# First feed-forward stage on the unnormalised state, and the last expert's down products by part

## The chip, the cores and the metric

The kernel runs on one core of one Trainium2 chip. The metric is the device time of one execution in microseconds (us); smaller is better. Engine names are those of the profile: PE (TensorE, with PEld its weight loads), DVE (VectorE), ACT (ScalarE), POOL (GpSimd), SP (SyncE, which issues most DMAs).

## The reference

Two transformer blocks, each of two layers, over 256 tokens of width 1024 in fp32. Only two places of it matter here.

The first is the dense feed-forward stage of layer 0:

```python
def rmsnorm(x, g):
    y = x * lax.rsqrt(jnp.mean(x * x, axis=-1, keepdims=True) + EPS)
    return y * g

h = rmsnorm(x, norm_ffn[0])
x = x + (silu(h @ wg) * (h @ wu)) @ wd      # width D_FF = 2816
```

For one token the root is one number, so `h @ wg` is `(x * g) @ wg` times that token's root.

The second is the end of the mixture of experts in layer 1: eight experts of width 3584, each token goes to two of them, and the gated sum of the experts' down products is added to x. A fused norm (the final norm of the first block and the first norm of the second) and another dense feed-forward stage follow.

## The kernel before

The state `xT` lies with the model width in the partitions: 8 blocks k of 128 rows by T = 256 tokens. Every product of two fp32 matrices is made from parts: a value is split into a high part (ACT copies it to fp32r) and a low part (DVE subtracts the high part), and PE adds hi*hi, hi*lo and lo*hi. So weights pass through three engines: SP loads a tile into a ring of four slots, ACT makes `w_hi`, DVE makes `w_lo`, PE multiplies. The work of each engine is written out by hand in program order, and semaphores join the engines.

**A dense feed-forward stage.** `norm(n)` comes first. ACT squares the 8 blocks of xT (L774), POOL adds them in pairs (L620), PE sums over partitions with a matrix of ones into `SS`, bank 6 of PSUM (L2131), ACT makes the inverse root by a logarithm and an exponential (L759, L760) into `norm_s`. DVE multiplies each block of xT by its gains and the root to `hT` (`scaled`, L1340), ACT copies it to `a_hi` (`split_input`, L830), DVE subtracts to `a_lo` (`rest`, L1357). PE runs six matmuls into bank 7 that nobody reads (L2135) behind the sums. `head` (L754, L1312) splits the first weight tile of the stage early, `second` (L824, L1328, L1387) the second one in two halves: half 0 before the root, half 1 behind the root and the input's split.

`ffn` then runs over 22 chunks c of 128 hidden columns. PE: `up(c)` is 16 pairs of matmuls (L2510 with 512 columns, L2512 with 256) for gate and up into two banks, 4 and 5 for even c, 6 and 7 for odd c; then `down(c-1)`, 24 matmuls of 256 columns (L2106 to L2108) into banks 0 to 3. ACT in a chunk: the high part of the next up tile (L1117), of this down tile (L1126), the copy of half of the up sums out of PSUM (L1132), Silu (L1138). DVE in a chunk: the low part of the next up tile (L1691), of this down tile (L1700), in most chunks one or two blocks of a matrix-vector product for the second block of the model (L1682, one in chunks 1 to 4, two in chunks 5 to 20), the addition of the two halves of the sums (L1710), the product of Silu(gate) and up (L1717), its high and low part (L1720, L1722). `up(c+1)` needs L1691, `down(c)` needs L1722. ACT's L1117 for the tile after next stands behind the Silu of the chunk. In chunk 21 the next stage's first half tile is split (L1312) in place of L1691. The stage of this change is `ffn(0)`, behind `norm(1)`.

**The end of the experts.** The last expert has 28 chunks too, n = 196 to 223. `down(n)` is six matmuls of 512 columns (L2673): high hidden by high weights, high by low, low by high, each for two halves of the output. At the end `down(223)` waits for DVE's low part of the last down tile (L1781), ACT and DVE each copy one half of the result to `ye` (L1265, L1922), PE waits for both, `scatter_last` (L2697) multiplies by the scatter matrix, DVE adds to xT (L1927), and `norm(5)` and `ffn(2)` follow. In the chunk before the last, DVE splits both halves of the head tile of `ffn(2)`.

Of the kernel before, what the change touches and what calls it, by code (L numbers as in the profile page):

```python
# [112 lines left out]
def build(nc, x_in, wstream, astream, crow, wpool, wrouter, vectors, consts, out):  # L113
# [6 lines left out]
    with ctx:  # L120
# [143 lines left out]
        gu_copied = sem("gu_copied")  # L264
        gu_added = sem("gu_added")
        sg_ready = sem("sg_ready")
        hid_ready = sem("hid_ready")
# [57 lines left out]
        xdown_done = sem("xdown_done")  # L325
        ye_ready = sem("ye_ready")
        ys_ready = sem("ys_ready")
        ys_added = sem("ys_added")
# [169 lines left out]
        def last_bank(j):  # L498

            return 2 * ((NE - 1 + j // 2) % 2) + j % 2  # L500

# [238 lines left out]
        def _(act):  # L740
# [21 lines left out]
            def norm(n):  # L762
# [6 lines left out]
                if n == 5:  # L769
                    act.wait_ge(both_roots, 1)  # L770
                for k in range(KB):
                    if n:
                        act.wait_ge(x_ready, KB * (n - 1 - (n == 5)) + k + 1)
                    nc.scalar.activation(sq[:, k, :], xT[:, k, :], ACT.Square,  # L774
                                         scale=both[:, KB + k:KB + k + 1] if n == 5 else D ** -0.5)\
                        .then_inc(sq_ready, 1)
                if early and HEADS[n] not in FFN_STAGE:
                    head(n, 1)
                if n in SECOND_AT:
                    second(n, 0).then_inc(second_hi, 1)  # L780
# [13 lines left out]
                if n in HEADS:  # L794
                    if n == 0:
                        head(n, 1)
                    act.sem_inc(hi_ready, 1 if HEADS[n] in FFN_STAGE else 2)
                if n < 3:
                    split_input(f"n{n}", hT, h_ready, KB * n)
                elif n >= 5:  # L800
                    for k in range(KB):
                        act.wait_ge(normed, KB * (n - 5) + k + 1)
                        if k == 0:
                            act.wait_ge(mod_done, MOD_BATCH[n])
                        shift = mod[:, (n - 5) // 3, 3 * ((n - 5) % 3) * KB + k:
                                    3 * ((n - 5) % 3) * KB + k + 1]
                        nc.scalar.activation(a_hi[:, k, :], sq[:, k, :], ACT.Identity, bias=shift)\
                            .then_inc(ah_ready, 1)
                        if n == 5:
                            nc.scalar.activation(hT[:, k, :], xT[:, k, :], ACT.Square).then_inc(final_sq, 1)  # L810
# [385 lines left out]
            def moe_fast():  # L1196
# [65 lines left out]
                nc.scalar.preload_act_table_set("natural_log_exp_and_others")  # L1262
                act.wait_ge(xdown_done, NE * FX + 2)
                act.wait_ge(ye_out, ROWS_OUT[NE - 1])
                nc.scalar.activation(ye[0:CAP, 0:512], ps[0:CAP, 2 * ((NE - 1) % 2), :], ACT.Copy).then_inc(ye_ready, 1)  # L1265

# [36 lines left out]
        def _(dve):  # L1303
# [11 lines left out]
            def norm(n):  # L1315
# [6 lines left out]
                if n in (2, 6, 9):  # L1322
                    head(n, 1)
                if n in SECOND_AT:
                    stage = HEADS[n]
# [6 lines left out]
                if n == 3:  # L1332
                    up_lo_half(0, 0, 0)
                    nc.vector.memset(rt[:, 1, 0, :], 0.0).then_inc(mask_ready, 1)
                dve.wait_ge(norm_root, norm_at(n) + 1)

# [22 lines left out]

                if n == 3:  # L1360
                    for k in range(KB):
# [312 lines left out]
            def ffn(f, n):  # L1674
# [10 lines left out]
                def chunk(c, r=0, last=False, blocks=()):  # L1685
# [19 lines left out]
                    for i in blocks[:1]:  # L1705
# [4 lines left out]
                    nc.vector.tensor_tensor(sm[:, b::2, :], sm[:, b::2, :], gu[:, :, 0:T], ALU.add)\  # L1710
                        .then_inc(gu_added, 1)
                    for i in blocks[1:]:
# [120 lines left out]
            def moe_fast():  # L1833
# [38 lines left out]
                def expert(n_e, r, last=False):  # L1872

                    for c in range(FX):
# [14 lines left out]
                        elif c == FX - 2:  # L1889
                            head(5, 0)  # L1890
                            head(5, 1)
                        for half in range(2):
# [28 lines left out]
                dve.wait_ge(ye_out, ROWS_OUT[NE - 1])  # L1921
                nc.vector.tensor_copy(ye[0:CAP, 512:1024], ps[0:CAP, 2 * ((NE - 1) % 2) + 1, :]).then_inc(ye_ready, 1)  # L1922
                dve.wait_ge(ys_added, 3)
                for j in range(KB // 2):
# [172 lines left out]
        def _(pe):  # L2097
# [26 lines left out]
            def norm(n):  # L2124
# [7 lines left out]
                ins.then_inc(ss_ready, 1)  # L2132
                if n in HEADS:
                    for _ in range(6):
# [354 lines left out]
            def ffn(f, n, norm_n):  # L2489
# [3 lines left out]
                def up(c, r=0):  # L2493
# [5 lines left out]
                    for k, g in [(k, g) for k in range(KB) for g in range(2)] if c < 2 else \  # L2499
                            [(k, g) for g in range(2) for k in range(KB)]:  # L2500
                        if c == 0 and g == 0:
                            wait_head(norm_n, k)
# [129 lines left out]
            def moe_fast():  # L2632
# [29 lines left out]
                def down(n, r):  # L2662
# [13 lines left out]
                    ins.then_inc(xdown_done, 1)  # L2676

                def turn_rows(n_e, half):

# [14 lines left out]
                def scatter_last():  # L2694

                    for d in range(KB):
                        ins = mm(ps[:, last_bank(d // 2), (d % 2) * T:(d % 2 + 1) * T], ye[0:CAP, d * P:(d + 1) * P],  # L2697
                                 scatter[0:CAP, :], start=d % 2 == 0, stop=True, skip_group_check=True)
# [43 lines left out]
                expert(NE - 1, 0, last=True)  # L2742
                down(NE * FX - 1, 0)
                pe.wait_ge(ye_ready, 2 * NE)
                pe.wait_ge(ys_added, 3)
# [14 lines left out]
            mixer1(0, 0)  # L2760
            norm(1)
            ffn(0, FF, 1)
# [158 lines left out]
```

## Time and profile before

| | us |
|---|---|
| median of 3 runs (2436.2 to 2438.71) | 2437.72 |
| time of the profiled execution | 2436.53 |
| span of its profile | 2434.8 |
| PE busy | 2410.2 (99%) |
| DVE busy | 2043.3 (84%) |
| ACT busy | 1512.0 (62%) |
| POOL busy | 177.6 (7%) |

The granted TensorE clock is 0.999 over the span. The profile lists for each engine what it did and when, and for each idle stretch which engine's work ended it. Times of a timeline are counted from the start of the span. Matmuls are pipelined: the duration of one record is longer than the distance to the next one, and it is the distance that counts in a row of them. A product of two plain fp32 operands shows as two records.

### The profile page before, as it was taken

How to read it: one execution, taken by the hardware profiler on the slowest of the kernel's cores; microseconds unless marked ns; L12 is line 12 of the kernel's file. 1: busy time of each engine (PE TensorE's matmuls, PEld its weight loads, DVE VectorE, ACT ScalarE, POOL GpSimd, SP SyncE). 2: the span in 40 equal slices, each digit the busy share in tenths (PEclk: the TensorE clock that was granted, in tenths of full speed). 3: DMA queues.
4: the chain of work that ended last, by engine and by line, in shares of the span. 5: the costliest groups of instructions: out<-in, count | busy, mean ns of one | idle time of the engine just before them, and what ended most of it. 6: DMA issues, size and time to landing. Idle time of an engine off the chain costs nothing.

```text
span 2434.8 us, 43980 instructions
## 1 busy us (share of the span) xinstructions
PE 2410.2 (99%) x17072; PEld 2199.2 (90%) x17072; DVE 2043.3 (84%) x2623; ACT 1512.0 (62%) x2091; POOL 177.6 (7%) x244
## 2 busy tenths in 40 slices
PE   9999999999999999999999999999999999999999
PEld 9999999998999999899988899988999899988998
DVE  5688867999999999999998899787888888787665
ACT  5644565777787778778876544567544544566443
POOL 2211020100000000000010111011011010010000
PEclk9999999999999999999999999999999999999999
DMA  7698554999999999999998788433787687432551
GB/s 290 229 354 313 193 186 182 387 391 379 371 399 416 374 383 399 405 370 392 402 416 334 259 312 298 152 130 122 285 319 277 233 320 286 147 122 95 208 185 76
DMA packets 135662, 693.51 MB, mean 285 GB/s; under 512 B 16113, under 2 KB 16241, under 8 KB 86769
## 3 DMA queue, kind: packets, MB, share of 16 engines
q1 hardware_dynamic: 109872, 598.79, 64.8%
q0 software_dynamic: 23280, 87.17, 9.3%
q10 hardware_dynamic: 2304, 4.72, 0.5%
q8 instruction: 139, 2.28, 0.4%
q14 instruction: 67, 0.54, 0.1%
HBM read 681.98 MB, written 11.40 MB: 285 GB/s over the span
## 4 chain that ended last, share of the span: by engine, by line
PE 90%; DVE 5%; ACT 3%; issue 1%; DMA 0%; POOL 0%; DVEq 0%; ACTq 0%; SPq 0%; POOLq 0%
PE ps L2510 17%; PE ps L2106 16%; PE ps L2107 16%; PE ps L2108 16%; PE ps L2673 11%; PE ps L2512 9%; DVE w_parts L1387 1%; PE ps L2131 1%; PE ps L2135 1%; PE ps L2638 1%; DVE w_parts L1774 1%; ACT w_parts L838 1%; DMA ring<-wstream 0%; DVE xT L1409 0%; PE ps L2378 0%
## 5 line engine op out<-in xcount | busy, mean ns | idle before, releaser
L2510 PE MATMUL ps<-a_parts,w_parts 128*128 128x512 f32 x1760 | 618.7, 393 | 1.4 <-DVE a_parts L1352 1.0
L1774 DVE TENSOR_TENSOR w_parts<-ring,w_parts 128x2048 fp32r<-128x2048 f32 x221 | 506.5, 2292 | 51.0 <-ACT w_parts L1161 44.0
L2106 PE MATMUL ps<-w_parts 128*96 128x256 f32 x1792 | 501.5, 280 | 1.1 <-DVE w_parts L1774 1.0
L2108 PE MATMUL ps<-w_parts 128*96 128x256 f32 x1792 | 498.3, 278 | 0.0
L2107 PE MATMUL ps<-w_parts 128*96 128x256 f32 x1792 | 498.0, 278 | 0.0
L2512 PE MATMUL ps<-a_parts,w_parts 128*128 128x256 f32 x1760 | 492.6, 280 | 0.0
L1161 ACT ACTIVATE w_parts<-ring 128x2048 fp32r<-128x2048 f32 x221 | 422.7, 1913 | 1.5 <-DMA ring<-wstream 1.3
L2510 PEld LDWEIGHTS ps<-a_parts,w_parts 128*128 128x128 f32 x1760 | 329.8, 187 | 75.3 <-issue 3.5
L2512 PEld LDWEIGHTS ps<-a_parts,w_parts 128*128 128x128 f32 x1760 | 332.4, 189 | 0.0
L2106 PEld LDWEIGHTS ps<-w_parts 128*96 128x96 f32 x1792 | 288.0, 161 | 27.0 <-issue 17.7
L2107 PEld LDWEIGHTS ps<-w_parts 128*96 128x96 f32 x1792 | 288.4, 161 | 9.0
L2108 PEld LDWEIGHTS ps<-w_parts 128*96 128x96 f32 x1792 | 288.1, 161 | 0.0
L1781 DVE TENSOR_TENSOR a_parts<-ring,a_parts 128x1024 fp32r<-128x1024 f32 x224 | 271.3, 1211 | 0.0
L1132 ACT ACTIVATE sm<-ps 128x512 f32<-128x512 f32 x110 | 65.4, 595 | 329.4 <-PE ps L2512 329.4
L2673 PE MATMUL ps<-a_parts,hid_hi 128*96 128x512 f32 (+1 forms) x896 | 259.8, 411 | 1.1 <-DVE a_parts L1781 1.1
L1691 DVE TENSOR_TENSOR w_parts<-ring,w_parts 128x2048 fp32r<-128x2048 f32 x100 | 229.3, 2293 | 28.3 <-ACT w_parts L1117 26.9
L2108 PE MATMUL ps<-hid_hi,w_parts 128*128 128x256 f32 x880 | 249.0, 283 | 0.0
L2106 PE MATMUL ps<-hid_hi,w_parts 128*128 128x256 f32 x880 | 247.4, 281 | 1.5 <-DVE hid_lo L1722 1.5
L2107 PE MATMUL ps<-hid_lo,w_parts 128*128 128x256 f32 x880 | 248.9, 283 | 0.0
L1167 ACT ACTIVATE a_parts<-ring 128x1024 fp32r<-128x1024 f32 x224 | 235.3, 1050 | 1.1 <-PE ps L2673 1.1
L2106 PE MATMUL ps<-a_parts,w_parts 128*128 128x256 f32 x784 | 229.7, 293 | 1.1 <-DVE a_parts L1357 0.7
L2107 PE MATMUL ps<-a_parts,w_parts 128*128 128x256 f32 x784 | 221.7, 283 | 0.0
(283 smaller groups left out, 4370.1 us busy)
## 6 DMA issues: line engine op xcount, KB each, us to landing
ring<-wstream SPq DMA_DIRECT2D x378, 1024.0 KB, 7.4
ring<-wstream SPq DMA_DIRECT2D x378, 512.0 KB, 7.0
proj<-astream POOLq DMA_DIRECT2D x144, 512.0 KB, 5.5
slot_rows<-branch POOLq DMA_DIRECT2D x7, 384.0 KB, 6.2
slot_out<-slot_rows POOLq DMA_DIRECT2D x1, 2688.0 KB, 11.7
sq<-slot_rows ACTq DMA_DIRECT2D x36, 64.0 KB, 5.5
slot_out<-pT ACTq DMA_DIRECT2D x36, 64.0 KB, 5.3
vtok<-crow POOLq DMA_DIRECT2D x3, 512.0 KB, 3.8
```

Source lines behind the costliest of these rows:

```text
L1132: nc.scalar.activation(sm[:, c % 2::2, :], gu[:, :, T:2 * T], ACT.Copy).then_inc(gu_copied, 1)
L1161: nc.scalar.activation(up_hi[:, n % 2, :], ring[:, s, 0:UP], ACT.Copy).then_inc(xup_hi, 1)
L1167: nc.scalar.activation(wd_hi[:, n % 2, :], ring[:, s, UP:TILE], ACT.Copy).then_inc(xdown_hi, 1)
L1691: nc.vector.tensor_tensor(w_lo[:, (q0 + c + 1) % 2, 0:UP], ring[:, (i0 + c + 1) % NS, 0:UP], w_hi[:, (q0 + c + 1) % 2, 0:UP], ALU.subtract)\
L1774: nc.vector.tensor_tensor(up_lo[:, n % 2, :], ring[:, s, 0:UP], up_hi[:, n % 2, :], ALU.subtract).then_inc(up_used, 1)
L1781: nc.vector.tensor_tensor(wd_lo[:, n % 2, :], ring[:, s, UP:TILE], wd_hi[:, n % 2, :], ALU.subtract).then_inc(signal, 1)
L2106: mm(o, stationary[0], moving[0], start=start, stop=False, skip_group_check=True)
L2107: mm(o, stationary[0], moving[1], start=False, stop=False, skip_group_check=True)
L2108: return mm(o, stationary[1], moving[0], start=False, stop=stop, skip_group_check=True)
L2510: mm(ps[:, bank, :], hi, a_parts[:, :, k, :], start=k == 0, stop=k == KB - 1, skip_group_check=True)
L2512: ins = mm(ps[:, bank, 0:T], lo, a_hi[:, k, :], start=False, stop=k == KB - 1, skip_group_check=True)
L2673: ins = mm(ps[0:rows, bank + half, :], h[:, b, 0:rows], w[:, b, half * D // 2:(half + 1) * D // 2], start=c == 0 and i == 0, stop=c == FX ...
```

## The change

In `norm(1)`:
- ACT squares blocks 0 to 5; once all eight blocks of xT are ready it writes `a_hi` directly from xT, scaled by the norm gains; then come squares 6 and 7. DVE makes `a_lo` as xT times gains minus `a_hi`. `hT` is not written; neither waits for the root.
- PE's five matmuls of the sum over partitions move from ahead of the stage into `up(0)`, ahead of its pair (6, 0), that is behind 12 of 16 pairs. The six matmuls into bank 7 go. `up(1)`, whose banks include bank 6, waits for the root.

In `ffn(0)`, in each of 22 chunks, DVE multiplies the sums of gate and up (128x512, in place) by the root, between L1710 and Silu, with a wait for L1710's own end.

At the end of the experts:
- `down_last` replaces the last `down`: the four products with the high weights run ahead of the wait for the low part of the weights, and each half signals by itself (`xhalf_done`, `xdown_done`).
- ACT copies half 0 as soon as it is complete and PE scatters it, and waits for DVE's copy of half 1 only ahead of the fifth block. The banks of the scatter are taken in the order 2, 0, 1, 3.
- DVE's split of half 1 of the head tile of `ffn(2)` moves from the chunk before the last to behind DVE's copy of half 1.

```diff
-            return 2 * ((NE - 1 + j // 2) % 2) + j % 2
+            return (2, 0, 1, 3)[j]
...
-                for k in range(KB):
+                for k in range(6 if n == 1 else KB):
...
+                if n == 1:
+                    act.wait_ge(x_ready, KB)
+                    for k in range(KB):
+                        nc.scalar.activation(a_hi[:, k, :], xT[:, k, :], ACT.Identity, scale=V("norm_ffn", k))\
+                            .then_inc(ah_ready, 1)
+                    for k in range(6, KB):
+                        nc.scalar.activation(sq[:, k, :], xT[:, k, :], ACT.Square, scale=D ** -0.5)\
+                            .then_inc(sq_ready, 1)
...
-                if n < 3:
+                if n in (0, 2):
                     split_input(f"n{n}", hT, h_ready, KB * n)
...
-                act.wait_ge(xdown_done, NE * FX + 2)
+                act.wait_ge(xhalf_done, 1)
                 act.wait_ge(ye_out, ROWS_OUT[NE - 1])
-                nc.scalar.activation(ye[0:CAP, 0:512], ps[0:CAP, 2 * ((NE - 1) % 2), :], ACT.Copy).then_inc(ye_ready, 1)
+                nc.scalar.activation(ye[0:CAP, 0:512], ps[0:CAP, 2 * ((NE - 1) % 2), :], ACT.Copy).then_inc(ye_half, 1)
...
+                if n == 1:
+                    for k in range(KB):
+                        dve.wait_ge(ah_ready, KB * e + k + 1)
+                        nc.vector.scalar_tensor_tensor(a_lo[:, k, :], xT[:, k, :], V("norm_ffn", k), a_hi[:, k, :],
+                                                       ALU.mult, ALU.subtract).then_inc(as_ready, 1)
...
                     nc.vector.tensor_tensor(sm[:, b::2, :], sm[:, b::2, :], gu[:, :, 0:T], ALU.add)\
-                        .then_inc(gu_added, 1)
+                        .then_inc(gu_raw if f == 0 else gu_added, 1)
+                    if f == 0:
+                        if c == 0:
+                            dve.wait_ge(norm_root, norm_at(1) + 1)
+                        dve.wait_ge(gu_raw, c + 1)
+                        nc.vector.tensor_tensor(sm[:, b::2, :], sm[:, b::2, :],
+                                                norm_s[:, 1, :].unsqueeze(1).broadcast_to([P, 2, T]), ALU.mult)\
+                            .then_inc(gu_added, 1)
...
                             head(5, 0)
-                            head(5, 1)
...
                 nc.vector.tensor_copy(ye[0:CAP, 512:1024], ps[0:CAP, 2 * ((NE - 1) % 2) + 1, :]).then_inc(ye_ready, 1)
+                head(5, 1)
...
-                if n in HEADS:
+                if n in HEADS and n != 1:
                     for _ in range(6):
...
+                        if f == 0 and c == 0 and (k, g) == (6, 0):
+                            norm(1)
+                        if f == 0 and c == 1 and (k, g) == (0, 0):
+                            pe.wait_ge(norm_root, norm_at(1) + 1)
...
+                def down_last(n):
+                    b, bank = n % 2, 2 * (n // FX % 2)
+                    def product(h, w, half, stop):
+                        return mm(ps[0:CAP, bank + half, :], h[:, b, 0:CAP], w[:, b, half * D // 2:(half + 1) * D // 2],
+                                  start=False, stop=stop, skip_group_check=True)
+                    pe.wait_ge(xhid_lo, n + 3)
+                    for half in range(2):
+                        product(hid_hi, wd_hi, half, False)
+                        product(hid_lo, wd_hi, half, False)
+                    pe.wait_ge(tile_used, STARTS[MOE_STAGE] + n + 1)
+                    product(hid_hi, wd_lo, 0, True).then_inc(xhalf_done, 1)
+                    product(hid_hi, wd_lo, 1, True).then_inc(xdown_done, 1)
...
                     for d in range(KB):
+                        if d == KB // 2:
+                            pe.wait_ge(ye_ready, 2 * NE - 1)
...
-                down(NE * FX - 1, 0)
-                pe.wait_ge(ye_ready, 2 * NE)
+                down_last(NE * FX - 1)
+                pe.wait_ge(ye_half, 1)
...
             mixer1(0, 0)
-            norm(1)
             ffn(0, FF, 1)
```

## Rows read from the trace of the kernel before

**Rows 1.** The page, busy time, share and instructions of each engine.

```profile
PE 2410.2 (99%) x17072; PEld 2199.2 (90%) x17072; DVE 2043.3 (84%) x2623; ACT 1512.0 (62%) x2091; POOL 177.6 (7%) x244
```

**Rows 2.** Timeline of PE: start, us, line, tiles, count, [idle before <-what ended it].

```profile
103.86 2.75 PE L2135 MATMUL ps<-cst,ones 128*128 128x256 f32 x12
106.56 0.47 PE L2510 MATMUL ps<-a_parts,w_parts 128*128 128x512 f32 x1
...
118.02 0.28 PE L2106 MATMUL ps<-hid_hi,w_parts 128*128 128x256 f32 x1
...
120.89 0.43 PE L2510 MATMUL ps<-a_parts,w_parts 128*128 128x512 f32 x1
```

**Rows 3.** Timeline of DVE from the last additions to xT on.

```profile
101.49 0.75 DVE L1407 TENSOR_TENSOR xT<-xT,ps 128x256 f32<-128x256 f32 x2
...
105.98 0.43 DVE L1357 TENSOR_TENSOR a_parts<-hT,a_parts 128x256 fp32r<-128x256 f32 x1
...
118.48 2.29 DVE L1691 TENSOR_TENSOR w_parts<-ring,w_parts 128x2048 fp32r<-128x2048 f32 x1 [1.61 <-ACT w_parts L1117]
```

**Rows 4.** Timeline of ACT: the root, and the second tile's half 1.

```profile
104.06 0.47 ACT L759 ACTIVATE pT<-ps,vec 128x256 f32<-128x256 f32 x1 [0.43 <-PE ps L2131]
104.57 0.42 ACT L760 ACTIVATE pT<-pT 128x256 f32<-128x256 f32 x1
...
110.83 1.04 ACT L824 ACTIVATE w_parts<-ring 128x1024 fp32r<-128x1024 f32 x1
```

**Rows 5.** Timeline of ACT, eight squares scaled by per-partition values, in norm(5).

```profile
1336.13 3.41 ACT L774 ACTIVATE sq<-xT,both 128x256 f32<-128x256 f32 x8 [2.20 <-DVE xT L1927]
```

**Rows 6.** Groups of DVE by shape: busy us, mean ns | idle before.

```profile
L1433 DVE TENSOR_TENSOR sm<-sm,small 128x512 f32<-128x512 f32 x8 | 5.5, 692 | 0.3
```

**Rows 7.** Timeline of DVE, one whole round of ffn(0).

```profile
157.39 2.29 DVE L1691 TENSOR_TENSOR w_parts<-ring,w_parts 128x2048 fp32r<-128x2048 f32 x1
...
160.97 1.23 DVE L1682 SCALAR_TENSOR_TENSOR proj<-proj,vtok 128x1024 f32<-128x1024 f32 x1
...
165.10 2.29 DVE L1691 TENSOR_TENSOR w_parts<-ring,w_parts 128x2048 fp32r<-128x2048 f32 x1
```

**Rows 8.** Timeline of DVE, chunks 20 and 21 of ffn(0).

```profile
279.18 0.69 DVE L1710 TENSOR_TENSOR sm<-sm,ps 128x512 f32<-128x512 f32 x1 [0.64 <-ACT sm L1132]
...
282.17 2.29 DVE L1312 TENSOR_TENSOR w_parts<-ring,w_parts 128x2048 fp32r<-128x2048 f32 x1
...
287.61 0.69 DVE L1710 TENSOR_TENSOR sm<-sm,ps 128x512 f32<-128x512 f32 x1 [2.02 <-ACT sm L1132]
...
289.25 0.29 DVE L1720 CAST hid_hi<-sm 128x256 fp32r<-128x256 f32 x1
289.57 0.43 DVE L1722 TENSOR_TENSOR hid_lo<-sm,hid_hi 128x256 fp32r<-128x256 f32 x1
```

**Rows 9.** Timeline of PE, the start of the last down product of ffn(0).

```profile
290.06 0.38 PE L2106 MATMUL ps<-hid_hi,w_parts 128*128 128x256 f32 x1 [0.30 <-DVE hid_lo L1722]
```

**Rows 10.** Timeline of PE at the end of the experts.

```profile
1330.46 0.62 PE L2673 MATMUL ps<-a_parts,hid_lo 128*96 128x512 f32 x2
1331.68 1.15 PE L2673 MATMUL ps<-a_parts,hid_hi 128*96 128x512 f32 x4 [0.61 <-DVE a_parts L1781]
...
1334.08 3.72 PE L2697 MATMUL ps<-proj,pT 96*128 96x256 f32 x16 [0.78 <-DVE pT L1922]
```

**Rows 11.** Timeline of DVE: the low part of the last down tile.

```profile
1330.33 1.22 DVE L1781 TENSOR_TENSOR a_parts<-ring,a_parts 128x1024 fp32r<-128x1024 f32 x1
```

**Rows 12.** Windows: length, busy (x) of PE, PEld, DVE, ACT, POOL; clock; DMA.

```profile
390.00:392.00 2.00, 2.00 (x20) 2.00 (x20) 1.11 (x3) 1.00 (x2) 0.00 (x0) 0.95 0.00 0
392.00:394.00 2.00, 2.00 (x11) 1.77 (x10) 1.44 (x9) 0.60 (x1) 0.00 (x0) 0.50 0.00 0
394.00:396.00 2.00, 2.00 (x13) 1.81 (x12) 1.88 (x7) 1.50 (x3) 0.00 (x0) 0.70 0.00 0
...
2433.00:2434.80 1.80, 0.00 (x0) 0.00 (x0) 0.00 (x0) 0.00 (x0) 0.00 (x0) 0.50 0.52 200
```

More of the change, by code:

```diff
@@ L265, in build @@
         gu_added = sem("gu_added")
+        gu_raw = sem("gu_raw")
         sg_ready = sem("sg_ready")
@@ L326, in build @@
         ye_ready = sem("ye_ready")
+        xhalf_done = sem("xhalf_done")
+        ye_half = sem("ye_half")
         ys_ready = sem("ys_ready")
@@ L1334, in norm @@
                     nc.vector.memset(rt[:, 1, 0, :], 0.0).then_inc(mask_ready, 1)
-                dve.wait_ge(norm_root, norm_at(n) + 1)
+                if n != 1:
+                    dve.wait_ge(norm_root, norm_at(n) + 1)
                 def scaled(k):
@@ L1358, in rest @@
                                                 ALU.subtract).then_inc(as_ready, 1)
-                if n == 3:
+                if n == 1:
+                    dve.sem_inc(h_ready, KB)
+                elif n == 3:
                     for k in range(KB):
```

## The prediction, made before the changed kernel was run

> **What bounds the kernel now.** I read the page's busy times first. PE is busy for 99% of the span [rows 1], so an edit gains only where it closes one of PE's few gaps and loses only where it opens one. Then I read the timelines of PE, DVE and ACT side by side at the two places of the change, and DVE's through the whole stage, since the edit adds DVE work to all 22 chunks. The reader should see two things. At the head of `ffn(0)` PE is filled with unread matmuls from 103.86 until 106.56 [rows 2]; this is where the root's chain costs time. And DVE is no spare engine there: a round of a chunk with two matrix-vector blocks takes it 7.71 (157.39 to 165.10) without a pause [rows 7], while PE's round is 8.43 (L1710 from 279.18 to 287.61) [rows 8]. DVE has 0.72 to spare per round. In the later rounds the spare time shows as a wait of 0.64 ahead of L1710 [rows 8]; early in the stage there is none, as DVE is still catching up.
>
> **Part 1, the head of the stage.** The last additions to xT end at 102.24 [rows 3]. `a_hi(0)` by ACT with a per-partition scale: eight such operations take 3.41, 0.43 each in a row, about 0.5 for one alone [rows 5], so 102.8. `a_lo(0)` on DVE takes 0.43 to 0.48, so 103.3, and PE starts 0.15 after it, as it did (106.41 to 106.56) [rows 2, 3]: 103.4 instead of 106.56, 3.1 earlier. Further blocks come each 0.43, PE needs four matmuls or 0.7 for one, so it doesn't wait again. The unread matmuls cost nothing when they go; they filled a wait.
> The sums now stand inside `up(0)`: 10 records, at 2.75 for 12 about 2.3 [rows 2]. Net on PE: 0.8 to 0.9 earlier at the end of `up(0)` and `up(1)`. The 32 pairs of both took 11.46 (106.56 to 118.02), 0.358 a pair [rows 2]; the sums start behind 12 pairs at 107.7 and end at 110.0. The root takes 0.93 [rows 4] and is there at 111.0, ahead of `up(1)` at about 111.4, so the new wait on bank 6 costs nothing. But ACT's half 1 of the second tile stands behind the root: 111.0 instead of 110.83 [rows 4], 0.2 later. From there to L1691 at 118.48 [rows 3] the same ACT and DVE instructions follow in the same order, none waiting for PE, plus the new product between L1710 and Silu.
>
> **Part 2, the product.** It is 128x512, plain fp32, in place with a broadcast operand: 0.69, as L1433 of that shape [rows 6]. It waits for L1710's end: such a successor starts 0.03 after it (L1720 ends at 289.54, L1722 starts at 289.57) [rows 8]. Silu comes 0.72 later. For DVE's own round: without a wait the next one overlaps by about 0.08 (two additions in 0.75) [rows 3], so the lost overlap is 0.11 and the product occupies 0.61: again 0.72. Bounds: 0.55 with no price for the wait and full overlap, 0.85 if the two-operand read from SBUF is disturbed.
> So L1691 of chunk 1 starts at 118.48 + 0.2 + 0.72 = 119.4 and ends at 121.7; `up(2)`, at 120.89 before [rows 2], starts at 121.8. The gain of 0.9 has turned into a loss of 0.9: PE comes early and waits.
> From here DVE sets the pace. Five rounds from 118.48 to 157.39 took 38.91, and now 3.6 more; so the round that began at 157.39 [rows 7] begins at 161.9. The next 15 take 7.71 + 0.72 = 8.43, the same as PE's own. DVE's lag is therefore never made up. Its work for chunk 21 (L1312) starts at 161.9 + 15 x 8.43 = 288.35 instead of 282.17 [rows 8], and at the same time PE starts `down(20)`, which was waiting for the hidden part just finished.
>
> **Part 3, the end of the stage.** Before, DVE was ahead here by 2.02 and waited for PE and ACT [rows 8]. Now it is the last: the two subtractions take 3.58 to what follows [rows 7], so L1710 at 291.9; from L1710 to the end of L1722 it was 2.39 (287.61 to 290.00) [rows 8], now 3.11, so 295.05, and PE starts `down(21)` 0.06 later [rows 9], at 295.1 instead of 290.06. PE has nothing in between: `down(20)` of 24 matmuls (2.87, 118.02 to 120.89 [rows 2]) is over at 291.3, so it stands idle for 3.8. The residual, norm(2) and all that follows hang on this product and move with it: **+5.1**. SP's ring loads and POOL's loads also follow DVE's lag, but each slot is loaded two rounds or more before its use, so I take 0 (0 to +0.5).
>
> **Part 4, the last expert.** `down(222)`'s last two records start at 1330.46, 0.23 apart (six in 1.4), so the array is free at 1330.9; `down(223)` started at 1331.68, after L1781's end at 1331.55 [rows 10, 11]. Its four products without the low weights take 0.93, to 1331.8, by when these are there: 0.8 saved. Half 0 is complete one matmul before half 1: 0.2. ACT's and DVE's copies run in parallel as before, PE begins after the first, and half 1's is in time for the fifth block, 1.8 later (16 records in 3.72 [rows 10]). The sums of norm(5) follow on PE without a gap, ACT's squares (3.41 [rows 5]) are shorter than scatter and sums together. DVE's moved split (1.2, as L1781 [rows 11]) fits between its copy and the first addition, which waits 0.9 for PE, up to 0.3 late; it then catches up, as squares aren't last. **-1.0** (-1.2 to -0.6).
>
> **Sum.** +5.1 - 1.0 = +4.1. On the profiled execution's 2436.53 this gives 2440.6; the median of the runs shown is 1.2 above that execution, so I forecast 2437.72 + 4.1 = 2441.8. A measurement tells this kernel from no change at about 0.2%, or 4.9 us: the forecast lies inside.
>
> **A. Forecast, +4.1 (2441.8), chance 0.45.** By itself it spreads over +2.5 to +5.5.
>
> **B. The idle 3.8 ahead of `down(21)` costs TensorE's clock too.** The granted clock falls from full to half (2.4 to 1.2 GHz) in two places of the rows: at the end of the span, where PE does nothing more (0.50 from 2433 on), and from 391 to 395, behind a wait and very small matmuls [rows 12]. There the three windows lack (0.05 + 0.50 + 0.30) x 2 = 1.7 of full-speed time. Here the half level would lie over `down(21)` and norm(2)'s sums, which wait in part anyhow: +1.4, so +5.5, 2443.2, slower. For it: no other gap of the stage is as long. Against: the waits around 1331 and 1334 [rows 10], up to 0.8 each, don't say what one of 3.8 does. Chance 0.25.
> The Trainium skill ("TensorE: Matmul & The Clock Gate", section "Why this matters for your kernels") advises against idle gaps between bursts of matmuls because the clock falls back; the rule speaks against this change and for B.
>
> **C. The wait for the own result is free.** Then the product adds 0.61 to DVE's round, which is 8.32, and DVE regains 0.11 in each of 20 rounds, 2.2 in all: +1.9, 2439.6. Against it: L1722's start 0.03 behind L1720's end, where unwaited ones overlap by 0.08 [rows 3, 8]. If a round were shorter by 0.17 or more, the lag would be gone by chunk 21 and +0.6 (2438.3) is left: 0.9 at the start and the product once at the end, less 1.0. Chance of both 0.13.
> The Trainium skill ("VectorE: DVE Perf Modes", section "The DRAIN you can't avoid") says that a semaphore between chained operations costs nothing extra; by it C would hold, while the rows named there speak against it.
>
> **D. The product is hidden throughout, and both heads gain:** -0.9 - 1.0 = -1.9, 2435.8, not slower. For it: the wait of 0.64 ahead of L1710 in late rounds [rows 8] could swallow 0.64 of 0.72. Against: early there is no such wait, and L1691 ended at 120.77, 0.12 ahead of `up(2)` [rows 2, 3]. Chance 0.07.
>
> **E. The rounds grow longer than PE's.** At 0.85 for the product each of 20 rounds is 0.13 longer and PE follows DVE: +2.6, in all +6.7, 2444.4, slower. It decides from about +0.05 a round. For it: DVE and ACT now both have rounds of 8.43, and any hitch on either adds up. Against: rounds so far agree within 0.01 [rows 7, 8]. Chance 0.10.
>
> **From cases to numbers.** Slower by over 0.2%: about a fifth of A, 0.7 of B, nearly all of E: 0.37. Faster by over 0.2% needs -4.9, more than D has: 0.02. Within: 0.61. The range, 2438.3 to 2444.6, leaves out D, half of C's lower end and the worst of E.
>
> **What would show it.** In the profile after: first L2510 of the stage at about 103.4; L1691 at 119.4 and `up(2)` at 121.8; products of 0.69 with Silu right behind; L1691 starts 8.43 apart from the first round on with no wait ahead of L1710; PE idle for 3 to 4 ahead of the last `down` of the stage, at about 295; the scatter 1.0 earlier relative to `down(222)`; clock at full (A) or half (B) behind 295. I am wrong if DVE waits for PE again in the late rounds (C, D), or if rounds are over 8.5 (E).

## The result, and the profile after

The changed kernel takes 2448.12 us (median of 5 runs, 2445.7 to 2450.49), the kernel before on the same chip 2438.71 (5 runs): ratio 1.0035, 95% interval [1.0023, 1.0048], so 9.4 us slower (5.6 to 11.7). In a second comparison, at the end of the study, it was 6.7 slower. The ratios in this document are estimates of their own and not quotients of the two medians: 1.0035 is 8.5 us. I had forecast 4.1 slower and a top of 2444.6; the time lies outside.

The profiled execution took 2445.7 (span 2444.0, before 2434.8). The root's ACTIVATE of each norm is a good milestone: it has one row in every trace. Between these roots the 9.2 of span splits so, each figure a difference of two distances:

```
stretch (of the profiled executions)               before   after   differ.
span start to the end of the last addition to xT   102.24   101.80   -0.44
from there to the root of norm(2)                  193.65   201.12   +7.47
root of norm(2) to root of norm(3)                  91.01    91.01    0.00
root of norm(3) to down(222)                       942.58   944.39   +1.81
down(222) to the root of norm(5)                    11.90    12.27   +0.37
root of norm(5) to the end                        1093.42  1093.41   -0.01
```

The first feed-forward stage holds most of it. The +1.81 is not the change's: four kernels of the study that are the kernel before in that stretch (e2, e7, e8, e9) have 945.3 to 947.0 there. A part of what differs is how long the half clock behind the router's wait lasts (windows of 0.50 from 398 to 404 in the changed kernel, one of them before [rows 12]). It isn't all: e2 has 947.0 with a half clock as long as the changed kernel's, and e12, the changed kernel again, has 943.8 with one as short as before. The rest is open.

PE's timeline of the changed kernel, at the head of the stage, answers to [rows 2]; columns as there.

```profile
103.00 0.47 PE L2540 MATMUL ps<-a_parts,w_parts 128*128 128x512 f32 x1 [2.00 <-DVE a_parts L1338]
...
108.81 2.32 PE L2157 MATMUL ps<-sq,ones 128*128 128x256 f32 x10
118.89 0.39 PE L2132 MATMUL ps<-hid_hi,w_parts 128*128 128x256 f32 x1 [0.83 <-DVE hid_lo L1748]
122.79 0.50 PE L2540 MATMUL ps<-a_parts,w_parts 128*128 128x512 f32 x1 [0.76 <-DVE w_parts L1710]
```

PE starts up(0) at 103.00, but now behind an idle of 2.00, where the kernel before had filled its wait with unread matmuls. The windows of the changed kernel show the price (length, busy of PE, PEld, DVE, ACT, POOL; clock; DMA):

```profile
103.00:104.00 1.00, 1.00 (x5) 0.88 (x6) 1.00 (x4) 1.00 (x4) 0.70 (x3) 1.00 0.00 0
104.00:105.00 1.00, 1.00 (x5) 0.90 (x4) 1.00 (x4) 1.00 (x3) 1.00 (x3) 0.59 0.55 152
105.00:106.00 1.00, 1.00 (x5) 0.81 (x5) 0.66 (x2) 1.00 (x4) 1.00 (x3) 0.50 0.81 238
106.00:107.00 1.00, 1.00 (x4) 0.86 (x4) 0.27 (x1) 0.70 (x1) 1.00 (x3) 0.50 0.96 262
107.00:108.00 1.00, 1.00 (x6) 0.85 (x4) 0.96 (x1) 0.00 (x0) 0.46 (x1) 0.70 0.91 279
```

The granted clock falls to half (1.2 of 2.4 GHz) for the stretch in which 12 pairs of up(0) should bring PE to the sums. The sums start 5.8 behind up(0), where 12 pairs at full clock take 4.3 (0.358 each), and with them everything that needs the root. ACT's timeline of the changed kernel, to be held beside [rows 4]:

```profile
111.17 0.47 ACT L762 ACTIVATE pT<-ps,vec 128x256 f32<-128x256 f32 x1 [4.47 <-PE ps L2157]
111.67 0.42 ACT L763 ACTIVATE pT<-pT 128x256 f32<-128x256 f32 x1
111.99 1.04 ACT L835 ACTIVATE w_parts<-ring 128x1024 fp32r<-128x1024 f32 x1
```

DVE's timeline of the changed kernel: the start of its first round, its last full round, and chunk 21. It answers to [rows 3, 7, 8].

```profile
120.45 2.29 DVE L1710 TENSOR_TENSOR w_parts<-ring,w_parts 128x2048 fp32r<-128x2048 f32 x1 [1.60 <-ACT w_parts L1128]
...
280.62 2.29 DVE L1710 TENSOR_TENSOR w_parts<-ring,w_parts 128x2048 fp32r<-128x2048 f32 x1
...
285.35 0.68 DVE L1729 TENSOR_TENSOR sm<-sm,ps 128x512 f32<-128x512 f32 x1
286.07 0.69 DVE L1735 TENSOR_TENSOR sm<-sm,pT 128x512 f32<-128x512 f32 x1
286.68 1.22 DVE L1701 SCALAR_TENSOR_TENSOR proj<-proj,vtok 128x1024 f32<-128x1024 f32 x1
...
289.06 2.29 DVE L1323 TENSOR_TENSOR w_parts<-ring,w_parts 128x2048 fp32r<-128x2048 f32 x1
...
292.70 0.69 DVE L1729 TENSOR_TENSOR sm<-sm,ps 128x512 f32<-128x512 f32 x1 [0.21 <-DVE w_parts L1719]
293.42 0.69 DVE L1735 TENSOR_TENSOR sm<-sm,pT 128x512 f32<-128x512 f32 x1
...
295.38 0.43 DVE L1748 TENSOR_TENSOR hid_lo<-sm,hid_hi 128x256 fp32r<-128x256 f32 x1
```

From 120.45 to 289.06 it is 20 rounds of 8.43, with no wait ahead of L1729 in the late ones. The product takes 0.69, and from L1729's start to the next block 1.33 pass, where the kernel before had 0.61. PE then waits for the last down product; its timeline and the windows behind it:

```profile
295.86 0.58 PE L2132 MATMUL ps<-hid_hi,w_parts 128*128 128x256 f32 x1 [3.48 <-DVE hid_lo L1748]
```

```profile
295.00:296.00 1.00, 0.14 (x1) 0.14 (x1) 0.90 (x5) 0.86 (x1) 0.00 (x0) 0.66 0.57 221
296.00:297.00 1.00, 1.00 (x5) 1.00 (x6) 0.68 (x10) 0.00 (x0) 0.00 (x0) 0.50 0.05 20
297.00:298.00 1.00, 1.00 (x7) 1.00 (x6) 0.45 (x2) 0.00 (x0) 0.00 (x0) 0.50 0.00 0
298.00:299.00 1.00, 1.00 (x7) 1.00 (x7) 0.47 (x2) 0.75 (x2) 0.17 (x1) 0.63 0.00 0
```

From down(21) to the root of norm(2) it is 7.06 now and was 5.83. The last expert, in PE's timeline of the changed kernel, answers to [rows 10]:

```profile
1338.32 1.14 PE L2703 MATMUL ps<-a_parts,hid_hi 128*96 128x512 f32 x4 [0.50 <-DVE a_parts L1807]
...
1341.76 3.72 PE L2745 MATMUL ps<-proj,pT 96*128 96x256 f32 x16 [0.46 <-ACT pT L1276]
1346.83 3.72 PE L2157 MATMUL ps<-sq,ones 128*128 128x256 f32 x16 [1.35 <-ACT sq L777]
```

The scatter comes 3.44 behind down(222) instead of 4.60, as forecast. But the sums of norm(5) follow it after a pause of 1.35 that the trace of the kernel before doesn't have: 5.07 behind the scatter's start instead of 3.56. The row names ACT's square, but ACT began its squares at 1343.85 and takes 0.42 for each (eight in 3.37), so the first had been there for over 2; something else ended this wait.

### The profile page after: what moved, and what is told of

It is laid out like the page before. It is cut to its first block, busy times and chain, and to the rows that moved or that the text cites. A ratio compares the mean times of both kernels' runs of the same rounds, so it can differ in the third digit from the quotient of the medians.

```text
span 2444.0 us, 43964 instructions
## 1 busy us (share of the span) xinstructions
PE 2411.8 (99%) x17060; PEld 2201.2 (90%) x17060; DVE 2054.5 (84%) x2637; ACT 1509.1 (62%) x2091; POOL 177.6 (7%) x244
## 4 chain that ended last, share of the span: by engine, by line
PE 83%; DVE 10%; ACT 4%; issue 2%; DMA 0%; POOL 0%; DVEq 0%; ACTq 0%; SPq 0%; POOLq 0%
PE ps L2132 15%; PE ps L2134 15%; PE ps L2133 15%; PE ps L2540 13%; PE ps L2703 11%; PE ps L2542 7%; DVE w_parts L1710 2%; DVE w_parts L1719 1%; DVE w_parts L1406 1%; ACT w_parts L1128 1%; PE ps L2157 1%; PE ps L2668 1%; DVE sm L1729 1%; DVE w_parts L1800 1%; PE ps L2161 1%
## 5 line engine op out<-in xcount | busy, mean ns | idle before, releaser
L1710 DVE TENSOR_TENSOR w_parts<-ring,w_parts 128x2048 fp32r<-128x2048 f32 x100 | 229.3, 2293 | 28.3 <-ACT w_parts L1128 26.9
```

What stands on the lines that cost most here:

```text
L1710: nc.vector.tensor_tensor(w_lo[:, (q0 + c + 1) % 2, 0:UP], ring[:, (i0 + c + 1) % NS, 0:UP], w_hi[:, (q0 + c + 1) % 2, 0:UP], ALU.subtract)\
```

## The experiments

All times are medians beside the kernel before on the same chip: 2439.23 for e1 to e4, 2439.25 for e5 to e8, 2438.47 for e9 to e11, 2440.00 for e12.

**e1 and e2, one half of the change each.**

e1 is the changed kernel with the edits of the last expert taken back, e2 the kernel before with only these. Their core, for e1 (in e2 the other way round):

```diff
-                down_last(NE * FX - 1)
-                pe.wait_ge(ye_half, 1)
+                down(NE * FX - 1, 0)
+                pe.wait_ge(ye_ready, 2 * NE)
                 pe.wait_ge(ys_added, 3)
                 scatter_last()
```

> The edits of norm(1) and ffn(0) alone, the experts' end as before. Theory: VectorE's lag (5.1) plus two stretches of half clock behind PE's new pauses (1.6 behind the 2.0 pause at the stage's start, which passes on to VectorE through the root, and 1.3 behind the 3.5 pause ahead of the last down product): +7 to +9 us against before, the spread being the router's stretch of half clock behind it, which differs by up to 1.6 between executions. Rival, that the experts' end carries a large share of the loss: +5 or less. L1691 of chunk 1 (or its line here) starts 2.4 later relative to the last addition to xT than before; chunks 8.43 apart.

> The edits of the experts' end alone. In the changed kernel the scatter began 1.16 earlier but the sums of norm(5) started 1.35 after the array was free. Theory 1, that this pause belongs to the edit (PE's instructions behind the branch arrive late): the pause shows again, 1 to 2 us between the end of the scatter and the sums, and the kernel is within 0.5 us of before. Theory 2, that the pause is a chance of that execution or comes from ffn(0)'s edits: no pause, and -1.0 to -1.2 us.

e1 takes 2447.14, ratio 1.0036 [1.0024, 1.0048]: as much as the whole change. e2 takes 2440.59, ratio 1.0000 [0.9991, 1.0009]: no difference, but the interval is 2.2 wide to either side, so the time alone can't tell the forecast -1.0 from nothing. Its trace can: the root of norm(5) comes 11.92 behind down(222), before 11.90. e2's timeline of PE has the early scatter and the pause again:

```profile
1336.98 3.72 PE L2717 MATMUL ps<-proj,pT 96*128 96x256 f32 x16 [0.46 <-ACT pT L1267]
1341.71 3.72 PE L2133 MATMUL ps<-sq,ones 128*128 128x256 f32 x16 [1.01 <-ACT sq L776]
```

So the pause belongs to the edit of the last expert and not to the later arrival there: it is 0.60 to 1.57 in all eight traces with the whole edit and PE's norm(5) behind the branch, and 0 and 0.14 in the two without the edit (before, e1). From down(222) to the root of norm(5) these eight have 11.52 to 12.49, 12.06 on average, and the two 11.90 and 12.21: what the earlier scatter gained is gone.

**e3, e4 and e11, what the clock costs.** Unread matmuls fill PE's idle at the start (e3), at the end (e11), or at both ends (e4) of the stage.

```diff
+            fill(7, 4)          # e3, e4
             ffn(0, FF, 1)
...
                 down(n - 2)
+                if f == 0:      # e4, e11
+                    fill(4, 8)
                 down(n - 1)
```

> The changed kernel with four unread matmuls (1.7 us) into bank 7 ahead of up(0), in the pause of 2.0. Theory (clock): no half clock inside up(0), the sums end 1.6 earlier, L1710 of chunk 1 starts 1.6 earlier, and the whole is 1.6 (1.0 to 2.2) us faster than the changed kernel, about +7.5 against before. Rival (VectorE's lag alone makes the loss and the clock only coincides): no difference to the changed kernel, +9.2.

> As the last, and eight unread matmuls (3.5 us) into bank 4 between down(20) and down(21) of ffn(0). Theory (clock): no half clock behind 295 either, the root of norm(2) 1.3 earlier relative to down(21), and 2.9 us (2 to 4) faster than the changed kernel, about +6 against before. Rival: no difference, or slower by the part of the eight that doesn't fit into the pause (up to 0.5).

> The changed kernel with eight unread matmuls between down(20) and down(21) of the first feed-forward stage, and nothing else. If the idle 3.5 ahead of down(21) costs by TensorE's clock: full clock there, 1.2 to 1.4 from the start of down(21) to the root of norm(2) saved (5.83 instead of 7.06 to 8.05), so 1.2 to 2.2 less time than the changed kernel, and the half clock at the start of the stage stays with its 1.5. If the clock doesn't matter there, as the additions wait for data, the time is that of the changed kernel within 0.5.

e3 takes 2443.67, ratio 1.0021 [1.0011, 1.0031]; e4 2443.43, 1.0018 [1.0009, 1.0027]; e11 2443.66, 1.0021 [1.0012, 1.0030]. These intervals are 2.2 to 2.4 wide to either side, too wide to tell steps of 1 or 2 between the three; the steps are read from the traces. In e3's timeline of PE the fill fits into the gap, and in ACT's the root comes 7.88 behind the end of the last addition to xT (102.93), where the changed kernel had 9.37:

```profile
101.98 1.89 PE L2369 MATMUL ps<-cst,ones 128*128 128x256 f32 x8
104.14 0.47 PE L2540 MATMUL ps<-a_parts,w_parts 128*128 128x512 f32 x1 [0.27 <-DVE a_parts L1338]
```

```profile
110.81 0.47 ACT L762 ACTIVATE pT<-ps,vec 128x256 f32<-128x256 f32 x1 [2.98 <-PE ps L2157]
```

The half clock at the start costs 1.5. Three expectations fell in part. e3 was to be about 7.5 over before and is 4.4 by the medians (5.1 by the ratio); its trace has 7.0 at the root of norm(2), but is that of its slowest execution (2448.64). Both fills together gave no more than either alone by the medians. And e11's own trace has no half clock at the start, though PE idles there for 1.99. Of six traces with that idle left open, three have it (the changed kernel, e1, e5: root at 9.37 to 9.40) and three haven't (e6, e11, e12: 7.80 to 7.81). Code that is the same up to there gets it in one execution and not in another. In all eight traces in which unread matmuls fill the wait (before, e2, e7, e8 and e9 with the old head, e3, e4 and e10) the clock stays full. e12's root, to be held beside the changed kernel's at 111.17, stands 7.81 behind its last addition (102.65):

```profile
110.46 0.47 ACT L762 ACTIVATE pT<-ps,vec 128x256 f32<-128x256 f32 x1 [2.90 <-PE ps L2157]
```

At the end all five traces with an open idle of 3.4 to 3.7 have half clock, and need 7.06 to 8.05 from down(21) to the root of norm(2) instead of 5.83: 7.06 and 7.09 in the two where the half level lasts for about 3 (the changed kernel, e6), 8.05 in the three where it lasts for about 7 (e1, e3, e12). The three traces with this idle filled (e4, e10, e11) have full clock and 5.83 or 5.84. In e4 DVE's L1748 starts at 294.69 and the root is at 301.00, which is the full-speed distance:

```profile
294.69 0.43 DVE L1748 TENSOR_TENSOR hid_lo<-sm,hid_hi 128x256 fp32r<-128x256 f32 x1
```

```profile
301.00 0.47 ACT L762 ACTIVATE pT<-ps,vec 128x256 f32<-128x256 f32 x1 [0.45 <-PE ps L2157]
```

Without half clock at either end, 198.31 pass from the last addition to the root of norm(2) in e4 and 198.37 in e11, against 193.65 in the kernel before: 4.7 remain, which the clock doesn't explain.

**e5, the product in chunk 0 alone.** The product is left out for chunks 1 to 21, so what this kernel computes isn't the reference's result.

```diff
-                    if f == 0:
-                        if c == 0:
-                            dve.wait_ge(norm_root, norm_at(1) + 1)
+                    if f == 0 and c == 0:
+                        dve.wait_ge(norm_root, norm_at(1) + 1)
```

> The changed kernel, but the multiplication by the root is left out for chunks 1 to 21 of the first feed-forward stage (chunk 0 keeps it), so gate and up sums of these chunks stay unscaled. Theory 1 (the product in DVE's round keeps DVE's lag, which is what the end of the stage pays for): rounds of DVE go back to 7.71, the lag is gone after some ten rounds, DVE waits ahead of L1729 in the late rounds, PE sets the pace from up(2) on, and down(21), at 295.86 in the changed kernel, comes at 291.0 to 291.5 with PE idle under 1 ahead of it, at full clock: 4.6 earlier and 1.3 more for the clock, about 2442.2 us (2441 to 2443.5). Theory 2 (most of the loss is made at the start of the stage, by its half clock and the late root, and is only carried on): down(21) comes no more than 1.5 earlier, 2446.5 us or more.

e5 takes 2441.74, ratio 1.0010 [1.0001, 1.0019]. The time that theory 1 gave holds to 0.5. DVE's timeline of e5 in a late round, and PE's at the last down product:

```profile
205.21 0.69 DVE L1729 TENSOR_TENSOR sm<-sm,ps 128x512 f32<-128x512 f32 x1 [0.64 <-ACT sm L1143]
205.81 1.22 DVE L1701 SCALAR_TENSOR_TENSOR proj<-proj,vtok 128x1024 f32<-128x1024 f32 x1
```

```profile
291.98 0.39 PE L2131 MATMUL ps<-hid_hi,w_parts 128*128 128x256 f32 x1 [0.30 <-DVE hid_lo L1747]
```

The waits of 0.64 and 0.30 are those of the kernel before [rows 8, 9]. From up(2) to down(21) it is 169.32 again, 173.07 with the products. The delay of up(2) stays, the 3.75 behind it are the products'. DVE's rounds tell how: before, the first eight take 7.70 to 8.16 and only then 8.43, as DVE makes up its lag there, and in e5 it does so again (7.70 to 8.26); with the products all 20 take 8.42 to 8.47.

**e6, the product on POOL** for chunks 2 to 20, with both of DVE's blocks behind the addition as its cover.

```diff
+                    nc.gpsimd.tensor_tensor(sm[:, c % 2::2, :], sm[:, c % 2::2, :],
+                                            norm_s[:, 1, :].unsqueeze(1).broadcast_to([P, 2, T]), ALU.mult)\
+                        .then_inc(gu_added, 1)
```

> The changed kernel, with the product of chunks 2 to 20 on POOL instead of DVE, both matrix-vector blocks of DVE placed behind L1729 as its cover, and POOL's loads of these blocks issued behind each product. POOL took 0.74 to 1.2 for an addition of 128x256, so 1.5 to 2.4 is an estimate for 128x512. Theory 1 (it is DVE's time that counts, not the chain's length): at up to 1.7 the two blocks (2.3) cover product and Silu, DVE's round is 7.7 to 7.8 again, and the end of the stage comes as in the kernel with one product: 2442.5 us. At 2.4 the round is 8.4 and nothing is gained: 2447 to 2449. Theory 2 (POOL and DVE hold each other up at SBUF): DVE's own operations grow from their 1.22 and 2.29 and the round passes 8.43: 2450 or more.

e6 takes 2455.85, ratio 1.0067 [1.0053, 1.0081], the slowest kernel of the study. DVE's and then POOL's timeline in one round:

```profile
212.79 1.22 DVE L1715 SCALAR_TENSOR_TENSOR proj<-proj,vtok 128x1024 f32<-128x1024 f32 x1
...
213.93 2.30 DVE L1715 SCALAR_TENSOR_TENSOR proj<-proj,vtok 128x1024 f32<-128x1024 f32 x1
```

```profile
212.96 2.20 POOL L718 TENSOR_TENSOR sm<-sm,pT 128x512 f32<-128x512 f32 x1 [4.78 <-DVE sm L1744]
```

POOL's product starts while DVE's first block runs and ends at 215.16, 1.15 behind that block's end; DVE's second block starts at 213.93, but ends 1.07 behind POOL's end. Read so that a record counts its wait for the other engine as busy, the three follow one another in 3.4 and don't overlap; DVE's second block takes 2.30 or 2.31 instead of 1.22 in all 16 rounds that have two blocks and a product on POOL, and the round grows to 8.91. Theory 2 holds. The Trainium skill ("SBUF — State Buffer", section "SBUF: two separate sides") describes this as a lock between DVE and GpSimd that is held for a whole instruction; the trace agrees.

**e7, e8 and e9, the pause behind the scatter.** All are e2 with one thing moved: PE's second wait to the head of the scatter (e7), DVE's split back to its old place (e8), PE's norm(5) into both branches of the MoE (e9).

```diff
                     for d in range(KB):
-                        if d == KB // 2:                          # e7
-                            pe.wait_ge(ye_ready, 2 * NE - 1)
...
+                pe.wait_ge(ye_ready, 2 * NE - 1)                  # e7, ahead of the scatter
...
                         elif c == FX - 2:
                             head(5, 0)
+                            head(5, 1)                            # e8
...
-                head(5, 1)                                        # e8
...
                 with nc.tensor.If(is_wide == 0):
                     moe_fast()
+                    norm(5)                                       # e9
                 with nc.tensor.Else():
                     moe_wide()
+                    norm(5)
```

> The kernel before with the edit of the last expert alone (2440.59 against 2439.23 for before on the last chip, with a pause of 1.01 ahead of norm(5)'s sums), and PE's wait for DVE's half moved from the middle of the scatter to its start. Theory 1 (the wait in the middle of the scatter holds PE's sequencer, so what lies behind the branch is fetched late): the pause ahead of the sums is under 0.2, the scatter starts 0.2 to 0.3 later, in all 0.7 to 0.9 faster than with the wait in the middle, 0.8 faster than before. Theory 2 (the fetch starts at a fixed place of the code or when the wait ahead of the scatter ends, and takes its 4 to 5 whatever PE does; the shorter idle ahead of the scatter only uncovers it): a pause of 0.8 to 1.3 stays and the time is that of before within 0.5.

> The kernel before with the edit of the last expert alone, but DVE's split head(5, 1) back at its old place ahead of the last rounds. Theory 1 (the pause ahead of norm(5)'s sums is PE's own, by its code): it stays at 0.6 to 1.4. Theory 3 (DVE's moved split delays the additions to xT, the squares and so the sums): the pause goes to under 0.2, and the kernel is 0.8 faster than the one with the edit alone.

> The kernel before with the edit of the last expert alone, and PE's norm(5) (sums and its six unread matmuls) issued at the end of both branches of the MoE instead of behind them. In nine traces norm(5)'s sums on PE started 2.5 to 3.2 behind the last of a pair of instruction-queue packets, which lie 5.0 to 5.4 behind the start of down(222) with and without the edit. Theory 1 (PE's instructions behind the end of the branch come late, and this ends PE's pause, not data): the sums now follow the scatter without a pause, about 7.1 behind the start of down(222) instead of 7.9 to 8.5, the wait for instructions moves behind the sums where the unread matmuls stood, and the time is 0.5 to 1.2 under that of the edit alone: 2438 to 2439 where before has 2439.2. Theory 2 (the pause is ended by data, squares or additions): it stays where it is, at 0.6 to 1.3, and so does the time.

e7: 2440.28, ratio 1.0000 [0.9991, 1.0009], pause 0.59. e8: 2438.23, ratio 0.9996 [0.9987, 1.0005], pause 0.77. Both pauses are smaller than e2's 1.01, neither goes; neither the wait in the middle nor the moved split alone is the cause. e9: 2439.53, ratio 1.0004 [0.9995, 1.0013]. Its timeline of PE:

```profile
1335.47 3.72 PE L2717 MATMUL ps<-proj,pT 96*128 96x256 f32 x16 [0.46 <-ACT pT L1267]
1339.03 3.62 PE L2133 MATMUL ps<-sq,ones 128*128 128x256 f32 x16
...
1350.78 0.50 PE L2512 MATMUL ps<-a_parts,w_parts 128*128 128x512 f32 x1 [1.99 <-issue]
```

The sums follow the scatter at once, with the same squares: data didn't end the pause. The root of norm(5) comes 10.65 behind down(222) instead of 11.90. But now PE stands still for 1.99 inside up(0) of the next stage, waiting for nothing that the profile shows, and from the root to the end it is 1094.62 instead of 1093.42. The gain moved the hole, and the time stayed. In the twelve traces with PE's sums behind the branch, the sums start 2.4 to 3.1 after the second of a pair of packets on the instruction queues (q14, q8), and the first of the pair lies 4.7 to 5.5 behind down(222), with the edit and without. That PE waits for its instructions behind the end of the branch fits all of this, but isn't shown; which event starts the fetch wasn't tried.

**e10, all mends on the changed kernel**: e4 with PE's norm(5) inside the branches.

> The changed kernel with four unread matmuls ahead of the first feed-forward stage, eight ahead of its down(21), and PE's norm(5) issued inside the branches. Theory 1 (DVE's lag at the end of the stage is what is left): root of norm(1) 7.8 behind the last addition to xT, root of norm(2) 190.5 behind it, still 5 over before; with the tail 0.5 to 1.2 better than with both fills alone: 2442.5 (2441.5 to 2443.5) where before has 2439.2. Theory 2 (the half clock is the cause of most of the loss and its last part was the pause in the tail): 2440 or less.

e10 takes 2448.29, ratio 1.0038 [1.0024, 1.0052], where theory 1 expected 2442.5. Up to the root of norm(5) it did what was expected: root of norm(2) 198.48 behind the last addition, 4.8 over before where 5 was expected (the 190.5 there is a slip of mine for 198.5), and 10.64 from down(222) to the root of norm(5). Then comes PE's row:

```profile
1354.73 0.37 PE L2542 MATMUL ps<-a_parts,w_parts 128*128 128x256 f32 x1 [4.42 <-issue]
```

The hole of e9 is 4.42 here, and 1099.29 pass from that root to the end, 5.9 more than in the kernel before. The same edit puts 1.0 behind that root when made on e2 and 5.8 when made on e4. Of the difference of 4.8 the longer hole is 2.4. Most of the rest is the clock, which e10's windows show at half behind the hole and e9's don't:

```profile
1352.00:1354.00 2.00, 0.00 (x0) 0.00 (x0) 2.00 (x5) 1.55 (x6) 0.80 (x2) 0.86 0.43 172
1354.00:1356.00 2.00, 1.27 (x5) 1.08 (x5) 1.67 (x3) 1.55 (x5) 0.79 (x2) 0.50 0.04 12
1358.00:1360.00 2.00, 2.00 (x8) 1.71 (x7) 0.98 (x1) 0.00 (x0) 0.00 (x0) 0.50 0.78 328
1360.00:1362.00 2.00, 2.00 (x13) 1.79 (x12) 0.00 (x0) 0.00 (x0) 0.00 (x0) 0.93 0.88 248
```

PE works at half clock from 1354.73 until past 1360, which costs it up to 2.8 (half of that time, an estimate). The two holes end at the same place, 18.75 (e9) and 18.86 (e10) behind down(222), but PE stops earlier in e10; why it stops earlier is open.

**e12, the changed kernel again.**

> The changed kernel once more, unaltered, since its first comparison gave +9.4 and its head edits alone +7.9 over before. From the steps that eleven traces show between the last addition to xT and the root of norm(2): 4.65 for DVE's lag at full clock, 1.55 for half clock at the start of the stage where a trace has it (three of five without unread matmuls there), 1.2 or 2.2 for half clock behind down(21), and 0 for the tail. If these are all there is, the median is 6 to 8.5 over before's; at 9 or more something that these steps don't hold is still missing. In the trace the root of norm(1) is 7.8 or 9.4 behind the last addition, down(21) 173.1 behind up(2), the root of norm(2) 7.1 or 8.1 behind down(21).

2446.71, ratio 1.0028 [1.0017, 1.0039], 6.7 over before, inside the 6 to 8.5. Its trace is one without half clock at the start: root of norm(1) 7.81 behind the last addition, down(21) 173.06 behind up(2), and 8.05 to the root of norm(2).

## Why the prediction was wrong

The forecast failed in three steps: two clock prices that it put at nothing, and the gain of the last expert.

**The clock at the head of the stage.** The first step that failed is the one which said of the removed unread matmuls at the head that they "cost nothing when they go; they filled a wait". They also held the clock. Without them PE idles for 2.0, and in three of six traces the clock is half for about 3 behind it: +1.5 on the root, which DVE's chain hands on undiminished, as I had worked out that its lag is never made up. I looked for a long idle at the end of the stage and not for the shorter one that I had made myself at its head.

**The clock at the end.** The second step is the forecast's own (case A): full clock behind the idle ahead of down(21), a price of nothing. It is the largest miss of the three. Case B had mechanism and place right, and about the price: +1.4 was said, 1.23 or 2.22 measured. It was given a chance of 0.25 and left out of the forecast; it came in all five traces in which the idle stayed open. The Trainium skill ("TensorE: Matmul & The Clock Gate", section "Why this matters for your kernels") warned of such gaps; here the trace agrees with it at the end of the stage. I should have made B the forecast.

**Part 1, by its own terms.** With full clock it holds: I put the root's row at 110.07 (111.0 less its 0.93), which is 7.83 behind the last addition, and e12 has 7.81, e3 7.88, e4 7.81.

**Part 2.** Product 0.69 (0.69), 0.72 more in a late round (8.43 against 7.71), late rounds of 8.43 (8.43), no wait ahead of L1729. Case C, the free wait, is out: the product starts 0.04 behind the end of the addition (286.03 to 286.07) and the round grows by 0.72, so the rule named beside C doesn't hold for this pair. D and E are out with it: nothing of the product is hidden, and the rounds stay at 8.43. up(2) was to come 0.9 later; it comes 0.8 later at full clock (19.44 behind the last addition in e12, 18.65 before).

**Part 3.** +5.1 said. At full clock e4 and e11 have 4.7. The 0.4 between is 0.1 at up(2), and for the rest the first five rounds: I gave them 38.91 + 3.6, or 8.50 each, and they take 8.43 like the others. PE's idle was to be 3.8 and is 3.44 to 3.53.

**Part 4.** The scatter's 1.16 earlier is there (1.0 was said), but the third step that failed is that the sums follow "without a gap": -1.0 turned into +0.4 in the changed kernel's trace, and into 0 on the average of eight traces. I had checked squares and additions as what the sums wait for, but not that a branch ends between scatter and sums. e9 shows that the pause isn't data's; that it is the supply of instructions is argued, not shown.

**The sum.** 4.7 for the lag, 1.23 to 2.22 for the clock at the end, 1.5 in three of six traces for that at the start, 0 for the tail: 5.9 to 8.4. Up to the root of norm(2) the traces add up: 4.7 + 1.5 + 1.23 = 7.4 in the changed kernel (7.47 measured), 4.7 + 2.22 = 6.9 in e12 (6.89), all three in e1 (8.4; 8.44). The two comparisons gave 9.4 (5.6 to 11.7) and 6.7 (4.1 to 9.5), e1 7.9. Their intervals hold the sum, and don't tell whether something of 1 or 2 is still missing in the first. Its middle, 7.2, is 3.1 over the forecast: 1.7 for the clock at the end, 1.0 for the tail and 0.8 on average for the clock at the start, less 0.4 in the lag. That it would be slower by over 0.2% I had given 0.37.

No version of the study beats the kernel before: e8 is 1.0 under it, with an interval that holds no change.

## What to carry to other kernels

A wait that is filled with unread matmuls can't be shortened by deleting them: count what stays idle, and what the clock behind it does to the next chain. An engine may need the spare time of its rounds to make up a lag from the start of the loop. Here DVE had 0.72 to spare in a round and the product took it all: the 22 products cost nothing round by round, but the lag stayed (4.7) and was paid once, where the loop ends and the other engine has nothing left to do. Look there first for the price and for the idle it opens. A gain just ahead of the end of a branch is worth nothing until the trace shows that the work behind the branch moves with it.

## What the runs showed that I had not expected

Idle of 2.0 on PE is followed by half clock in three of six traces of otherwise equal stretches (and not behind e9's hole of 1.99), idle of 3.4 to 3.7 in five of five, and so is e10's hole of 4.42. The half level lasts differently long over the same work: behind down(21) from about 295 to 299 in the changed kernel, from about 294 to 301 in e1. PE's hole behind the branch is 0 to 1.57 ahead of the sums and 1.99 or 4.42 where it falls among matmuls. And DVE's blocks and POOL's product take turns whole: 1.2 each, 3.4 for three.
